# Merging a mixer's two branches: y's high and low parts side by side, high weights in 512-column products, and the low products' sum added by VectorE

## What is computed

```python
gates = jax.nn.sigmoid(gl + b_gate).reshape(B, S, N_BRANCH, D)
merged = gates[:, :, 0] * (y_pool @ w_branch_pool) + gates[:, :, 1] * (y_attn @ w_branch_attn)
x = x + merged @ w_out
```

## Time and profile before

| | |
|---|---|
| median of 3 runs | 1437.62 us (1437.16 to 1437.67) |
| the profiled execution | 1437.53 us, of which 1435.7 us is the profile's span |
| TensorE busy | 1429.8 us, 100% of the span |
| VectorE busy | 984.9 us, 69% |
| ScalarE busy | 801.9 us, 56% |
| granted TensorE clock | 1.00 of full speed over the span |
| the three merges (first product to the first one of `finish`) | 300.16 to 334.16 us, and likewise in L1 and M |

### The profile page before, as it was taken

The page is one execution under the profiler, slowest core; times in us unless marked ns, Lnnn a source line. Parts: engine busy times, 40 slices in busy tenths (PEclk is TensorE's granted clock), DMA queues, the critical chain, the costliest instruction groups (busy, mean ns, idle before and its releaser), DMA issues.

```text
span 1435.7 us, 20811 instructions
## 1 busy us (share of the span) xinstructions
PE 1429.8 (100%) x8064; PEld 1232.6 (86%) x8064; DVE 984.9 (69%) x1601; ACT 801.9 (56%) x1409; POOL 144.6 (10%) x212
## 2 busy tenths in 40 slices
PE   9999999999999999999999999999999999999999
PEld 7888888898888888888888898888888899888887
DVE  6656676777666566666676677665676977778776
ACT  6545556754555555455566746554557765465553
POOL 0100024000000001000050004000038300100000
PEclk9999999999999999999999999999999999999999
DMA  8655555354655547555564455556646335456551
GB/s 337 247 192 189 191 204 192 133 186 164 222 186 186 198 140 244 189 193 190 176 233 140 156 190 202 183 188 198 194 156 233 131 119 188 161 170 216 193 188 59
DMA packets 73681, 267.76 MB, mean 187 GB/s; under 512 B 8176, under 2 KB 8304, under 8 KB 73456
## 3 DMA queue, kind: packets, MB, share of 16 engines
q1 hardware_dynamic: 73296, 265.65, 55.0%
q10 hardware_dynamic: 288, 0.79, 0.1%
HBM read 265.36 MB, written 1.05 MB: 186 GB/s over the span
## 4 chain that ended last, share of the span: by engine, by line
PE 99%; DMA 0%; DVE 0%; POOL 0%; issue 0%; POOLq 0%
PE bank L559 30%; PE bank L566 15%; PE bank L513 9%; PE bank L514 9%; PE bank L515 8%; PE bank L580 4%; PE bank L585 4%; PE bank L581 4%; PE bank L543 3%; PE bank L550 3%; PE bank L544 3%; PE bank L533 1%; PE bank L748 1%; PE bank L759 1%; PE bank L774 1%; PE bank L806 1%
## 5 line engine op out<-in xcount | busy, mean ns | idle before, releaser
L1630 DVE TENSOR_TENSOR wlo<-raw,whi 128x1024 fp32r<-128x1024 f32 (+1 forms) x481 | 579.7, 1228 | 14.6 <-ACT whi L1097 14.6
L1097 ACT ACTIVATE whi<-raw 128x1024 fp32r<-128x1024 f32 (+1 forms) x481 | 490.0, 1048 | 5.5 <-DMA raw<-w_dram 2.9
L559 PE MATMUL bank<-hx,whi 128*128 128x512 f32 x1856 | 452.4, 392 | 0.0
L559 PEld LDWEIGHTS bank<-hx,whi 128*128 128x128 f32 x1856 | 343.7, 188 | 71.1 <-issue 3.0
L566 PEld LDWEIGHTS bank<-hx,wlo 128*128 128x128 f32 x1856 | 242.0, 191 | 11.7
L566 PE MATMUL bank<-hx,wlo 128*128 128x256 f32 x1856 | 245.5, 282 | 0.0
L513 PE MATMUL bank<-whi,hid 128*128 128x512 f32 x536 | 211.2, 394 | 0.2 <-issue 0.2
L514 PE MATMUL bank<-wlo,hid 128*128 128x512 f32 x536 | 209.9, 392 | 0.0
L515 PE MATMUL bank<-whi,hid 128*128 128x512 f32 x536 | 208.6, 389 | 0.0
L1726 DVE TENSOR_TENSOR sil<-sil,bank 128x256 f32<-128x256 f32 x80 | 33.6, 420 | 182.0 <-ACT sil L1186 182.0
L1186 ACT ACTIVATE sil<-bank 128x256 f32<-128x256 f32 x80 | 30.5, 382 | 211.4 <-PE bank L566 211.4
(11 more groups left out here) (256 smaller groups left out, 1536.1 us busy)
## 6 DMA issues: line engine op xcount, KB each, us to landing
raw<-w_dram SPq DMA_DIRECT2D x486, 512.0 KB, 3.5
gain<-g_dram SPq DMA_DIRECT2D x7, 512.0 KB, 4.2
arena<-c_dram SPq DMA_DIRECT2D x2, 768.0 KB, 6.0
cst<-c_dram SPq DMA_DIRECT2D x1, 1056.0 KB, 5.9
out_dram<-x SPq DMA_DIRECT2D x4, 256.0 KB, 2.0
par<-p_dram SPq DMA_DIRECT2D x1, 867.0 KB, 7.5
raw<-w_dram SPq DMA_DIRECT2D x2, 432.0 KB, 3.1
gain<-g_dram ACTq DMA_DIRECT2D x1, 512.0 KB, 4.8
```

The source lines that it names most:

```text
L559: e.matmul(b[:, :], hi_of(j)[:, k * P:k * P + P], hx[:, k * 2 * S:k * 2 * S + 2 * S], start=k == 0, stop=False, skip_group_check=True)
L1097: e.activation(hi_of(t), raw_of(t), ACT.Copy).then_inc(sem["w_hi"], 1)
L1630: e.tensor_tensor(lo_of(t), raw_of(t), hi_of(t).bitcast(F32), ALU.subtract).then_inc(sem["w_lo"], 1)
```

## The change

- `yhi` and `ylo` become one tile `y`: for each of the 8 blocks the high part (256 columns) and the low part stand side by side. What writes them writes to the new places.
- For an output tile TensorE makes 8 products of 512 columns (whi by the high and low part of a block at once) and 8 of 256 columns (wlo by the high part). Each branch has a bank of its own: columns 0 to 255 gather high by high and low by high, columns 256 to 511 high by low. A tile so claims two banks, both ahead of its first product, and tile i + 2 gets the banks of tile i.
- ScalarE copies the right half of each bank to `sil` and `prod` (semaphore `br_low`). VectorE adds the left half to each (`br_sum`), which frees the bank. The gate products then read and write `sil` and `prod` in place.

```diff
@@ -297,7 +297,8 @@
                         claim((f"{tag}g", f, j), "g_sum", 16 * m + 2 * f + j + 1)
             ring = [0, 1, 2, 3]
             for i in range(KD):
-                claim((f"{tag}br", i), "mrg", 24 * m + 3 * i + 2)
+                for h in range(2):
+                    claim((f"{tag}br", i, h), "br_sum", 16 * m + 2 * i + h + 1)
...
         gates = sb("gates", KD * 2 * S)
-        yhi = sb("yhi", 8 * S, F32R)
-        ylo = sb("ylo", 8 * S, F32R)
+        y = sb("y", 16 * S, F32R)
...
-        yhi_of = lambda buf, blk: buf[:, blk * S:blk * S + S]
+        yhi, ylo = 0, 1
+        yhi_of = lambda part, blk: y[:, (2 * blk + part) * S:(2 * blk + part + 1) * S]
+        y_blocks = lambda part, b0, b1: y[:, :].rearrange("p (k j t) -> p k j t", j=2, t=S)[:, b0:b1, part, :]
+        by2 = lambda ap: ap.rearrange("p (k t) -> p k t", t=S)
...
@@ -809,17 +812,21 @@
             def merge_tail(s, m):
                 tag = STAGES[s]
                 for i in range(KD):
-                    b = claim((f"{tag}br", i))
+                    held = [claim((f"{tag}br", i, h)) for h in range(2)]
                     j = T[f"{tag}br{i}"]
-
-                    def pooled(k):
-                        if m < 2:
+                    E.wait_ge("w_hi", SI[j] + 1)
+                    for k in range(8):
+                        if k >= 4:
+                            E.wait_ge("yalo", 4 * m + k - 3)
+                        elif m < 2:
                             E.wait_ge("yplo", 4 * m + k + 1)
                         else:
                             E.wait_ge("m_ylo", 2)
-
-                    feat_block(j, b[:, 0:S], lambda k: hT(yhi, k), lambda k: hT(ylo, k), 4, 0, release=False, waits=pooled)
-                    feat_block(j, b[:, S:2 * S], lambda k: hT(yhi, 4 + k), lambda k: hT(ylo, 4 + k), 4, 1, waits=lambda k: E.wait_ge("yalo", 4 * m + k + 1))
+                        e.matmul(held[k // 4][:, :], hi_of(j)[:, k * P:k * P + P], y[:, 2 * k * S:2 * k * S + 2 * S], start=k % 4 == 0, stop=False, skip_group_check=True)
+                    E.wait_ge("w_lo", SI[j] + 1)
+                    for k in range(8):
+                        ins = e.matmul(held[k // 4][:, 0:S], lo_of(j)[:, k * P:k * P + P], yhi_of(yhi, k), start=False, stop=k % 4 == 3, skip_group_check=True)
+                    ins.then_inc(sem["tile"], 1)
                     if 3 <= i < KD - 1:
                         accum(s, i - 3)
                 finish(s, KD)
...
@@ -1312,6 +1319,12 @@
                         ahead(j)
                     else:
                         hi_upto(j + 4)
+                    mm = K.MUL0[s] + i
+                    E.wait_ge("tile", DONE[f"{tag}br{i}"])
+                    for h, dst in enumerate((sil[mm % 2], prod[mm % 2])):
+                        if mm >= 2:
+                            E.wait_ge(*(K.PROD_FREE if h else K.SIL_FREE)[mm - 2])
+                        e.activation(dst[:, :], bank[K.BANK[f"{tag}br", i, h][0]][:, S:2 * S], ACT.Copy).then_inc(sem["br_low"], 1)
                     E.wait_ge("mrg", 24 * m + 3 * i + 3)
                     hidden_hi(K.HID0[s] + i, prod[(K.MUL0[s] + i) % 2][:, :])
                     if 3 <= i < KD - 1:
...
@@ -1824,18 +1837,17 @@
                         ahead(j)
                     else:
                         lo_upto(j + 4)
-                    b = bank[K.BANK[f"{tag}br", i][0]]
                     g = [gates[:, (2 * i + k) * S:(2 * i + k + 1) * S] for k in range(2)]
                     mm = K.MUL0[s] + i
-                    sl = sil[mm % 2]
-                    if mm >= 2:
-                        E.wait_ge(*K.SIL_FREE[mm - 2])
+                    sl, pr = sil[mm % 2], prod[mm % 2]
                     base = 24 * m + 3 * i
-                    E.wait_ge("tile", DONE[f"{tag}br{i}"])
+                    for h, t in enumerate((sl, pr)):
+                        E.wait_ge("br_low", 16 * m + 2 * i + h + 1)
+                        e.tensor_tensor(t[:, :], t[:, :], bank[K.BANK[f"{tag}br", i, h][0]][:, 0:S], ALU.add).then_inc(sem["br_sum"], 1)
                     E.wait_ge("gate", 16 * m + 2 * i + 2)
-                    e.scalar_tensor_tensor(sl[:, :], g[0], 1.0, b[:, 0:S], ALU.add, ALU.mult).then_inc(sem["mrg"], 1)
-                    pr = prod_of(s, i)
-                    e.scalar_tensor_tensor(pr[:, :], g[1], 1.0, b[:, S:2 * S], ALU.add, ALU.mult).then_inc(sem["mrg"], 1)
+                    E.wait_ge("br_sum", 16 * m + 2 * i + 2)
+                    e.scalar_tensor_tensor(sl[:, :], g[0], 1.0, sl[:, :], ALU.add, ALU.mult).then_inc(sem["mrg"], 1)
+                    e.scalar_tensor_tensor(pr[:, :], g[1], 1.0, pr[:, :], ALU.add, ALU.mult).then_inc(sem["mrg"], 1)
                     E.wait_ge("mrg", base + 2)
                     e.tensor_tensor(pr[:, :], sl[:, :], pr[:, :], ALU.add).then_inc(sem["mrg"], 1)
                     hidden_lo(K.HID0[s] + i, pr[:, :])
```

More of the change, by code:

```diff
@@ L393, in build_program @@
                 "pT_ev", "low", "yahi", "gate", "k3_ev", "kc2_ev", "kT_ev", "nq_ev", "v3_ev", "mqk_ev", "lg_ln", "lg_ex", "c_part", "c_hc",
-                "c_kv", "c_exp", "c_pTe", "conv_t", "mv_ev", "ml_e", "ml_sq", "m_yhi", "mo_ev"]
+                "c_kv", "c_exp", "c_pTe", "conv_t", "mv_ev", "ml_e", "ml_sq", "m_yhi", "mo_ev", "br_low"]
         DVES = ["sq_v", "xhi0", "w_lo", "x", "xn", "xlo", "tok_m", "mul", "hidlo", "cv", "mrg", "hst_rd", "rp_n", "rp_c", "rp_add", "yplo",
-                "mx", "nrm", "g_sum", "yalo", "gfin", "sum", "lg_d", "lg_cp", "c_fold", "c_v", "c_s", "conv_q", "conv_k", "ml_k", "ml_p", "ml_d", "ml_n", "ml_g", "m_ylo", "gmo"]
+                "mx", "nrm", "g_sum", "yalo", "gfin", "sum", "lg_d", "lg_cp", "c_fold", "c_v", "c_s", "conv_q", "conv_k", "ml_k", "ml_p", "ml_d", "ml_n", "ml_g", "m_ylo", "gmo", "br_sum"]
         POOLS = ["mh", "rstd", "hb", "tab", "zero", "kst", "qst", "rp_s", "X", "warm", "cvp", "c_z", "ml_r", "padz", "rowz", "kz", "vz", "xz"]
@@ L1266, in y_hi @@
                 else:
-                    e.activation(yhi[:, (4 + 2 * c) * S:(6 + 2 * c) * S], side[3][:, :], ACT.Copy).then_inc(sem["yahi"], 2)
+                    e.activation(y_blocks(yhi, 4 + 2 * c, 6 + 2 * c), by2(side[3][:, :]), ACT.Copy).then_inc(sem["yahi"], 2)
             def attention(m, b, first, js):
@@ L1496, in mlstm_turned @@
                     E.wait_ge("tile", DONE[f"L1br{KD - 1}"])
-                    dst = yhi[:, 0:4 * S].rearrange("p (k t) -> p k t", t=S)[:, :, a * P:a * P + P]
+                    dst = y_blocks(yhi, 0, 4)[:, :, a * P:a * P + P]
                     e.activation(dst, by4(bank[2 + a][:, :]), ACT.Copy).then_inc(sem["m_yhi"], 1)
@@ L1802, in y_lo @@
                 else:
-                    two = lambda buf: buf[:, (4 + 2 * c) * S:(6 + 2 * c) * S]
+                    two = lambda part: y_blocks(part, 4 + 2 * c, 6 + 2 * c)
                     E.wait_ge("yahi", 4 * m + 2 * c + 2)
-                    e.tensor_tensor(two(ylo), side[3][:, :], two(yhi).bitcast(F32), ALU.subtract).then_inc(sem["yalo"], 2)
+                    e.tensor_tensor(two(ylo), by2(side[3][:, :]), two(yhi).bitcast(F32), ALU.subtract).then_inc(sem["yalo"], 2)
             def attention(m, b, first, js):
@@ L2081, in mlstm_lo @@
                     E.wait_ge("m_yhi", a + 1)
-                    dst = lambda buf: buf[:, 0:4 * S].rearrange("p (k t) -> p k t", t=S)[:, :, a * P:a * P + P]
+                    dst = lambda part: y_blocks(part, 0, 4)[:, :, a * P:a * P + P]
                     e.tensor_tensor(dst(ylo), by4(bank[2 + a][:, :]), dst(yhi).bitcast(F32), ALU.subtract).then_inc(sem["m_ylo"], 1)
```

## The result

| | before | after |
|---|---|---|
| median (range), 6 runs each | 1437.23 us (1437.10 to 1437.67) | 1442.65 us (1442.35 to 1443.13) |
| ratio of the times, 95% interval | | 1.0037 (1.0027 to 1.0048) |
| profiled execution, span | 1437.53, 1435.7 us | 1442.35, 1440.2 us |

Slower by 5.4 us, 0.4%. Forecast were 1442.2 us and slower. The profiled execution of after began its first merge 0.80 us earlier than that of before (299.36 against 300.16), where the two programs differ only in the places to which the branches' results are written. I therefore read stretches rather than the span.

The account below looks back on a forecast made before the run. TensorE, busy 100% of the span, was taken as the bound, with VectorE falling behind in the merges. Terms of 2 x 1.64 (L0, L1) + 1.30 (M) = +4.6 us on 1437.53 gave 1442.2, range 1437.2 to 1444.8.

Parts of the forecast that it names:

- TensorE's saving: Merge tiles on TensorE get 0.087 us shorter through wider products: 0.70 us a mixer, 2.09 for the kernel.
- VectorE's growth g: VectorE's cycle per merge tile grows by 0.83 us, from two additions and the gate product's wait for the second.
- the norm: Behind each merge, TensorE's transposes for the next norm come another 0.31 us late, waiting on VectorE.
- Late at TensorE: At L0's merge end, VectorE's low part of tile 7's `hid` lets TensorE resume 2.03 us late.
- M: Third mixer, whose merge starts with VectorE idle: 1.69 late, plus 0.31, minus 0.70, makes +1.30 us.
- The bank wait at tile 3: TensorE waits 0.2 us for tile 1's bank before tile 3; part of the 2.03 us delay, not additional.
- Weight splits stay 4 tiles ahead: no wait: In the merges, VectorE's weight splits never hold TensorE; the worst is done some 2.5 us early.
- Sensitivity: Each 0.01 us of VectorE's growth per tile costs 0.24 us over all three mixers.
- VectorE keeps up: Rival: no late `hid` in L0 if growth is under 0.59; only the saving remains, -2.1 us, 1435.5; chance 0.10.
- Half the wait: Rival: on VectorE a dependence costs nothing, growth 0.66 a tile; +0.5 us, 1438.1; chance 0.15.
- ScalarE sets the cycle: Rival: ScalarE's chain of high part, split and copy exceeds the merge cycle by 0.2; 4.8 us more, 1447.0; chance 0.12.
- Little saved: Rival: on TensorE a 512-column product costs twice a 256-column one, saving nothing; 2.1 us more, 1444.3; chance 0.03.

Follow-up runs that it names:

- e2: Changed kernel without ScalarE's copies and VectorE's additions; gate products read the banks' left halves, so part of the result is missing: 1434.63 us, ratio 0.9982.
- e9: Changed kernel with each tile's second bank claimed only ahead of product k = 4: 1442.49 us, ratio 1.0036.
- e10: Changed kernel with one more VectorE instruction per tile, ahead of the additions: 1448.34 us, ratio 1.0076.
- e1: Changed kernel with the joint wait split: first gate product waits for the first addition alone, second for the second: 1437.90 us, ratio 1.0005.
- e3: Changed kernel with each 512-column product cut into two of 256; copies and additions stay: 1442.88 us, ratio 1.0039.
- e4: Changed kernel with output tiles 0 to 2 of each merge in the old form, 3 to 7 new: 1439.69 us, ratio 1.0015.
- e7: e4 with the bank ring moved on three places behind each merge, so later stages get their former banks: 1437.09 us, ratio 0.9998.
- e11: e7 with the waits for the two additions apart; tiles 0 to 2 old, 3 to 7 new: 1436.49 us, ratio 0.9996.
- e12: As e11, but tiles 0 and 1 old and 2 to 7 new: 1435.65 us, ratio 0.9988.
- e13: e7 with the three skipped bank places ahead of the merge's claims instead of behind: 1440.55 us, ratio 1.0021.
- e8: Changed kernel with only tile 0 of each merge old, addition waits apart, ring moved on one place behind the merge: 1435.43 us, ratio 0.9987.

## Why the prediction was right, step by step

- **TensorE's saving.** 2.793 a tile forecast, 2.79 measured, and e2 gives it in full (0.78 a mixer; 0.70 forecast). The 10.9 ns for a merged pair held. The Trainium skill's spacing ("TensorE: Matmul & The Clock Gate", Back-to-back issue gap), which the page gives for isolated products and by which e2 would gain an estimated 0.5 us, does not hold for this stream: the three merges gained 2.3, the median 2.6.
- **VectorE's growth g.** 0.83 forecast, 0.87 measured: the second addition 0.34 behind the first, the gate product 0.52 behind that (0.50 forecast). The value lay within the near bounds of 0.77 and 0.89. Tile 7's addition came 36.57 behind the merge's start, forecast 36.33; the 0.24 are nearly all seven cycles of 0.04 more, less 0.03 at tile 0. *The term mis-sized is this one*, and with it the sum is +5.21 instead of +4.6. In L0: 0.27 from the cycles and 0.02 within tile 7, less 0.03 at tile 0 and 0.04 at the norm, make 1.86 of the forecast 1.64.
- **Late at TensorE.** Without waits the product was due 37.40 behind the merge's start, 336.76 here; it came at 339.05, 2.29 late (2.03 forecast). The forecast had this as one wait of some 2 us ahead of tile 7's product. It came in pieces: 0.30 at tile 3, 0.61 at the split below, 1.23 at tile 7's product, and 0.08 more for the first product behind each of the first two. From tile 7's addition to TensorE's start 3.12, forecast 3.10, in part by luck: TensorE starts 0.14 behind the low part's end, where the forecast took 0.05 and another 0.10 for the longer first product; what that product does cost, 0.08, falls behind its start and so into the 0.27. With 0.27 at the norm (0.31 forecast) and -0.70: 2.29 + 0.27 - 0.70 = 1.86, the stretch's growth. M: +1.50, forecast +1.30.
- **The bank wait at tile 3.** Forecast 0.2 within the whole, measured 0.30, and e9 shows that it is within.
- **"Weight splits stay 4 tiles ahead: no wait" was wrong,** and a wait of TensorE's for a weight split was one of the signs by which the prediction called itself wrong. The wait ahead of 334.97 is one: the product was due at 334.36, and VectorE began the split that it needs at 333.66, first of two that take 2.35. One takes 1.22, so it ended at 334.88. The profile names no releaser here; in e10, where the wait is longer, it names line 1643. I had counted how far ahead the splits stand in the order and not by how much VectorE, which makes them, falls behind. It cost nothing, since tile 7's `hid` comes later from the same queue; e10 has it at 1.71 and unpaid too.
- **Sensitivity.** 0.24 us for 0.01 of g forecast; e1 took 0.21 away and gained 4.75, e10 added 0.26 and lost 5.7: 0.23 and 0.22.
- **Rivals.** "VectorE keeps up" is excluded by e3 and e10. "Half the wait" is excluded as it stands, since the gate product came 0.52 behind the addition and not 0.33. It is what e1 built, and its price, 1438.1, was 0.2 off: right for other waits than the changed kernel has. "ScalarE sets the cycle": its copies were in time, the additions followed the splits at once, and e1 shortened the cycle by VectorE alone. "Little saved" is excluded by e2.

A reading that came out otherwise: I had put the extra time of a waiting instruction down to the number of its waits. e1 says that it matters whom it waits for. Then the Trainium skill's sentence that a semaphore costs nothing extra ("VectorE: DVE Perf Modes", The DRAIN you can't avoid) agrees with e1's row of 0.33 and not with the 0.44 to 0.52 of an instruction that waits for the one just ahead.

**Open:** the 0.3 to 1.9 us that e4 (beside the wait and the clock), e7, e11, e12 and e13 give back at stage M's start. Shown is where, and in e7 that a weight tile landed late and that less was moved in the microseconds from 1087 on; not why this is so in these kernels and not in e8. Nor is it the same in all of them: e12 has ScalarE wait 0.37 for a weight tile (1091.91) though 393 to 418 GB/s were moved from 1087 to 1090, and e11 has no such wait though it moved 172 in the first of these. No run took the transfers apart. Why the clock fell in e4 is open too.

## What to carry over

When work goes from the engine that is the bound to one with "30% free", compare the two cycles inside the stage, and follow the sum of the excess to the last tile; here 24 tiles of 0.087 us saved were paid with 24 of 0.87 on an engine that had 0.59 a tile to spare, by the bound that the prediction gives for "VectorE keeps up". Eight times the excess of 0.28 is 2.24, and 2.29 is how late L0's last product came. If you add instructions to such a chain, let each wait only for results older than the one just ahead: that alone was 4.75 us here. And if an edit changes how many buffers a stage claims from a ring that others go on with, look up where the later stages land: in e4 one new wait cost its own time and nearly as much again in clock.

## What the runs showed of the hardware that was not expected

- On VectorE, at 128 x 256 in float32: the next instruction starts 0.33 us behind one that it does not wait for, even with two waits in front of it for older results (e1); 0.44 to 0.45 behind one that it waits for (e10, and the earlier trace rows); 0.52 with a second, long fulfilled wait beside that one (after). By these rows a wait that has long been fulfilled costs 0.07 there, and in e1 nothing.
- TensorE's first product of 512 columns behind a wait lasted 0.47 to 0.50 instead of 0.39 to 0.40, and the next one came 0.08 later than in the stream (339.05 to 339.36 in after). It does not take a wait: behind the short transposes at 344.77 the product at 345.16 lasts 0.48 with no idle time ahead of it.
- In e4 TensorE's granted clock fell from 1.00 to 0.50 for some 3 us behind a standstill of 1.55 in the middle of the program, and that cost 1.5 us; in e10 it stayed at 1.00 behind one of 1.71.
- The same weight transfers, sent out at the same places of the program and 0.30 us apart in time, moved 188 to 295 GB/s in e7's execution and 385 to 414 in e8's, over the three microseconds from 1087.
